# One activation table for logarithm and exponential, loaded by hand, in a two-layer decoder trunk

## The chip, the cores and the metric

The kernel runs on one core of a Trainium2 chip. The metric is device time in microseconds (us), from the start of the program to its end. Lower is better.

## The reference

One inference step of a two-layer hybrid decoder, for a prompt of 1024 tokens and for 8 samples of 4 tokens each (1056 tokens in all), with D_MODEL = 1024. Layer 0 has gated DeltaNet heads and a spatial-gating group in parallel, layer 1 has mLSTM heads. Each layer ends in a squared-ReLU MLP of width 4096. Cut to what matters here:

```python
def rmsnorm(x, g):
    y = x * lax.rsqrt(jnp.mean(x * x, -1, keepdims=True) + EPS)
    return y * g
# layer 0
q, k = l2norm(silu(conv(q))), l2norm(silu(conv(k))); v = silu(conv(v))
beta = sigmoid(beta_pre); g = -exp(a_log) * softplus(a_pre + dt_bias)
decay = exp(gc_i - gc_j)                      # per chunk, and exp(gc), exp(gc_last - gc)
o_a = rmsnorm(o, gdn_norm_g) * silu(gate)
u = gelu(u_pre); vb = rmsnorm(gelu(v_pre), sgu_norm_g)
# layer 1
bcum = cumsum(log_sigmoid(f_pre)); w_intra = exp(dmat - m_t); w_inter = exp(inter - m_t)
hh = rmsnorm(h, head_norm_g) * sigmoid(o_pre)
# every layer
x = x + rmsnorm(mix, gl[1])
x = x + rmsnorm(jnp.square(relu(rmsnorm(x, gl[2]) @ w1)) @ w2, gl[3])
```

The kernel computes every reciprocal square root on ScalarE (ACT) as `exp(-0.5 * ln(mean + eps))`: one `Ln` and one `Exp`. Softplus and log-sigmoid are `Abs`, `Exp` and `Ln`.

## The kernel before, in words

The tokens are in two groups: group 0 has 512, group 1 has 512 and the 32 of the samples. Each dense product is cut into units of 128 output columns (128x1024 weights, 512 KB). Weights and inputs are float32, and each is split into a high part and a rest, so a product is three matmuls (high x high, rest x high, high x rest). For a unit, SyncE (SP) starts the transfer of the weights into `wst`, ACT writes the high part `whi` (`hi`, L936 to L942, a `Copy` of 128x1024), VectorE (DVE) subtracts it and writes `wlo` (L1355), and TensorE (PE) multiplies (L488, a helper through which all matmuls go). `wst`, `whi` and `wlo` have two buffers each.

The class `Plan` writes one order by hand, a list of items, and every engine runs through the same list and does its own share of each item, in that order. A unit is in the list as 4 pieces, `("d", unit, piece)`. Between the pieces stand the items of the token mixers, which run on 128 tokens at a time (`gdn`, L1125 to L1190, for layer 0; `ml`, L1242 to L1267, for layer 1), and of the norms (`square`, `norm_sum`, `pre`). No engine takes its work out of this order, so what ACT does for a mixer or a norm also delays the `whi` and the emptying of dense results that stand behind it in the list. Engines wait for each other by semaphores.

ACT applies one function table set at a time. The program names only the functions. When it is built, a load of a table set (`ACT_TABLE_LOAD` in the trace) is put in front of each activation whose function the set then loaded lacks, and of the sets that hold this function the first in the list is taken. The first set with `Exp` has no `Ln`, and the first set with `Ln` has no `Exp`. `Silu`, `Gelu` and `Sigmoid` are each in sets of their own. `Copy`, `Square`, `Relu` and `Abs` are in every set that this kernel loads. A set further down the list, `natural_log_exp_and_others`, holds both `Ln` and `Exp`.

Where the functions are used on ACT:

- Norms over the model width (`norm_sum`, 16 of them): `Ln` L1065, `Exp` L1068.
- Gates (`softplus`): `Exp` L1095, `Ln` L1096; `gdn_prep`: `Sigmoid` L1103, `Exp` L1106, L1110, L1112, L1113, L1115.
- Layer 0, nine tiles (8 of the prompt and the sample tile): `Ln` L1148 and `Exp` L1149, twice a tile (step "sum"); `Exp` L1152, `Ln` L1157, `Exp` L1159, L1161, L1163 (step "dec"); `Ln` L1199, `Exp` L1200 (`out_squares`). For the tiles of group 1 also `Silu` L1136, `Gelu` L1139 (step "act"), `Silu` L1142, `Gelu` L1143 (step "gact").
- The input product of layer 0, group 0: `Silu` and `Gelu` at L977, `Silu` at L981. That of layer 1: `Sigmoid` at L977.
- Layer 1, nine tiles: `Exp` L1248, L1250; `Ln` L1271, `Exp` L1272 (`head_rms`). `ml_prep`: `Exp` L1228, L1233.

All of them are called through the name `A_`, which in the kernel before is `act.activation` itself.

Of the kernel before, what the change touches and what calls it, by code (L numbers as in the profile page):

```python
# [8 lines left out]
ACT = mybir.ActivationFunctionType  # L9
# [271 lines left out]
def build(nc, x_prompt, x_sample, state_gdn, state_gdn_conv, state_mlstm_c, state_mlstm_n, state_mlstm_m,  # L281
# [4 lines left out]
    with ctx:  # L286
        sems = {}

        def S(name):
            if name not in sems:  # L290
                sems[name] = ctx.enter_context(nc.semaphore(name))
            return sems[name]
# [122 lines left out]
        def out_of(key, g):  # L415
            b = PLAN.jobs[key]["bank"]
            return DB[:, b:b + 2, 0:272] if g else DB[:, b, 0:512]

        def like(v, g):

            return v[:, 0:GN[1]].rearrange("p (a n) -> p a n", a=2) if g else v[:, 0:GN[0]]
# [27 lines left out]
        def evac_wait(eng, key):  # L449
            sem, v = PLAN.jobs[key]["read"]  # L450
            eng.wait_ge(S(sem), v)
# [3 lines left out]
        @block.sync  # L455
        def _(sp):
            def x_load(t):
                if t >= 4:
                    sp.wait_ge(S("x_turned"), t - 3)
                sp.dma_start(x_tm[:, t % 4, :], x_prompt[0, t * P:(t + 1) * P, :])\  # L460
                    .then_inc(S(f"x_loaded{t % 4}"), 16)

            for t in range(4):
                x_load(t)
            sp.dma_start(x_tm[0:NS, 4, :], x_sample.rearrange("b s d -> (b s) d")).then_inc(S("x_loaded4"), 16)
            for u, (kind, l, g, a, k) in enumerate(PLAN.units):
                dst = wst[:, u % 2, :]
                if kind == "f2":
                    src = w_ff2[l][a * FK * P:(a + 1) * FK * P, 2 * k * P:2 * (k + 1) * P]
                    src = src.rearrange("(t p) n -> p t n", p=P)  # L470
                else:
                    w = {"in": w_in[l][0], "out": w_out[l][0], "f1": w_ff1[l]}[kind] if kind != "f1" else w_ff1[l]
                    c0 = (a * FK + k) * P if kind == "f1" else a * P
                    if kind == "in" and a >= GATE0 // P:
                        c0 += 2 * H
                    src = w[:, c0:c0 + P].rearrange("(t p) n -> p t n", p=P)
                if u >= 2:
                    sp.wait_ge(S("w_split"), u - 1)
                sp.dma_start(dst.rearrange("p (a b) -> p a b", a=src.shape[1]), src)\
                    .then_inc(S(f"w_loaded{u % 2}"), 16)  # L480
                if u == 1:
                    for t in range(4, TILES):
                        x_load(t)

        @block.tensor
        def _(pe):
# [107 lines left out]
            def gate(l, g):  # L594
                begin(("gate", l, g))
                b = PLAN.jobs["gate", l, g]["bank"]
                if g == 0:
                    pe.wait_ge(S("wg_split"), l + 1)
                for i, t in enumerate(range(*GT[g])):
                    _, c, n = tok(t)  # L600
                    for k in range(KT):
                        for q, (x, w) in enumerate(((hhi, wg_hi), (hlo, wg_hi), (hhi, wg_lo))):
                            last = mm(DB[0:n, b, i * 8:(i + 1) * 8], x[g][:, k, c], w[:, k, :],
                                      start=k == 0 and q == 0, stop=k == KT - 1 and q == 2)
                last.then_inc(S("job_done"), 1)
# [173 lines left out]
            def ml_prep(g, i):  # L779
                if i == 1:  # L780
                    pe.wait_ge(S("m_g"), g + 1)
                    for j, t in enumerate(range(*GT[g])):
                        n = tok(t)[2]
                        for part in range(2):
                            b, c = (part, j * P) if t < TILES else (2, part * NS)
                            last = pe.transpose(MB[0:H, b, c:c + n], cols[0:n, t, part, :], ident[0:n, 0:n])
                    last.then_inc(S("m_rows"), 1)
                elif i == 5:
                    pe.wait_ge(S("m_lw"), g + 1)
                    for j, t in enumerate(range(*GT[g])):  # L790
                        _, c, n = tok(t)
                        for q, r in enumerate((AR, LWR, MR)):
                            last = pe.transpose(MB[0:n, 3, j * 12 + 4 * q:j * 12 + 4 * q + 4], r[0:H, c],
                                                ident[0:H, 0:H])
                    last.then_inc(S("m_cols"), 1)
                    pe.wait_ge(S("m_keep"), g + 1)
                    nk = 4 + g * NB
                    for h in range(H):
                        last = mm(MB[:, 2, h * (4 + NB):h * (4 + NB) + nk], spread(h), KPR[0:H, 0:nk])
                    last.then_inc(S("m_cols"), 1)  # L800
# [119 lines left out]

        @block.scalar
        def _(act):
            A_ = act.activation

            steps_done = [0]

            def own(ins):

# [7 lines left out]
            def hi(u):  # L936
# [4 lines left out]
                act.wait_ge(S(f"w_loaded{u % 2}"), 16 * (u // 2 + 1))  # L941
                A_(whi[:, u % 2, :], wst[:, u % 2, :], ACT.Copy).then_inc(S("w_hi"), 1)  # L942

# [3 lines left out]
            def in_end(u, l, g, c):  # L947
                i = PLAN.in_rank[u]
                b, n = i % 2, GN[g]
                if l == 0 and c < NCONV:  # L950
# [7 lines left out]
                    if c == 0:  # L958
                        evac_wait(act, ("misc", "par"))
                    A_(like(pout2[:, b], g), out_of((u, 0), g), ACT.Copy, scale=par[:, 100 + c:101 + c])  # L960
                    if g == 0:
                        last = A_(row[:, 3:3 + n], DB[:, bank, 0:n], ACT.Copy)
                    else:
                        A_(row[:, 3:275], DB[:, bank, 0:272], ACT.Copy)
                        A_(row[:, 275:515], DB[:, bank + 1, 0:240], ACT.Copy)
                        last = A_(row[:, 515:XR].rearrange("p (b s) -> p b s", b=NB)[:, :, 3:3 + LS],
                                  DB[:, bank + 1, 240:272].rearrange("p (b s) -> p b s", b=NB), ACT.Copy)
# [366 lines left out]
        def _(dve):  # L1334
# [29 lines left out]
            def h1_rest(u):  # L1364

                f = PLAN.ff1_rank[u]
                _, l, g, a, k = PLAN.units[u]
                n = GN[g]
                r = relu2[:, f % 2, 0:n]
                dve.wait_ge(S("h1_hi"), f + 1)  # L1370
                TT(h1lo[:, k, 0:n], r, h1hi[:, k, 0:n].bitcast(F32), ALU.subtract)\  # L1371
                    .then_inc(S("h1_split"), 1)
# [803 lines left out]
```

## Time and profile before

| | |
|---|---|
| median of 3 runs | 3125.89 us (3123.27 to 3126.25) |
| the profiled execution | 3117.21 us, its span 3115.5 us |
| PE busy | 2866.9 us, 92% of the span |
| weight loads on PE | 2560.4 us, 82% |
| DVE busy | 1420.0 us, 46% |
| ACT busy | 1293.5 us, 42% |
| mean granted clock of PE | 0.943 |
| HBM | 256.02 MB read, 54.91 MB written, 100 GB/s |

The span runs from the first to the last instruction of the profiled execution; 1.7 us of its time lie around it. "Busy" is the time in which an engine has an instruction running. "Idle before" a group of instructions is the time that the engine stood still just before them, and the name behind the arrow is what ended that wait. The granted clock is the share of full speed that PE was given.

### The profile page before, as it was taken

To read this page: it belongs to the slowest core of one execution; us is meant where nothing else is said; L and a number is where in the kernel's file an instruction comes from. 1 tells how busy PE (TensorE), PEld (TensorE's weight loads), DVE (VectorE), ACT (ScalarE), POOL (GpSimd) and SP (SyncE) were. 2 spreads that over 40 slices of the span, in tenths; PEclk is the share of its full clock that TensorE was granted. 3 is DMA by queue.
4 is the path that set the end of the run, shared out by engine and by line. 5 is a ranking of instruction groups with operands and counts; after the bars stand their busy time and mean duration, and the time that the engine had idled before them with its cause. 6 is when DMAs were issued, how large, how long until landed. Compare 5 with 4: busy or idle time off the path is not lost.

```text
span 3115.5 us, 41770 instructions
## 1 busy us (share of the span) xinstructions
PE 2866.9 (92%) x17557; PEld 2560.4 (82%) x17557; DVE 1420.0 (46%) x2129; ACT 1293.5 (42%) x2055; POOL 213.3 (7%) x348
## 2 busy tenths in 40 slices
PE   6989998869999998999999999999999889999995
PEld 5769898758787866888999998998777678899995
DVE  4543555455444443543444446443444435544334
ACT  3564443755535442444234334343343225433322
POOL 4010010100000000010000000010000100000000
PEclk7998998979999998989999999899999999999998
DMA  4442232313222222443332233354334544233222
GB/s 140 130 119 76 80 90 69 103 63 95 63 86 64 82 85 77 143 152 122 102 95 75 89 102 109 119 159 129 89 102 113 113 85 145 88 104 121 86 85 77
DMA packets 365354, 313.64 MB, mean 101 GB/s; under 512 B 11153, under 2 KB 338859, under 8 KB 365168
## 3 DMA queue, kind: packets, MB, share of 16 engines
q1 hardware_dynamic: 335024, 205.68, 23.7%
q0 software_dynamic: 30144, 105.30, 10.6%
q8 instruction: 139, 2.28, 0.3%
q14 instruction: 47, 0.39, 0.0%
HBM read 256.02 MB, written 54.91 MB: 100 GB/s over the span
## 4 chain that ended last, share of the span: by engine, by line
PE 75%; ACT 10%; DVE 8%; issue 3%; DMA 3%; POOL 0%; SPq 0%; ACTq 0%; DVEq 0%; POOLq 0%
PE dense L488 63%; PE mixer L488 10%; DVE wlo L1355 2%; ACT whi L942 1%; DVE ffh L1394 1%; DMA out_dram<-arena 1%; ACT L1148 1%; DMA wst<-in_w_out_odd_dram 1%; DVE hf L1477 1%; DMA wst<-in_w_ff_dram 1%; DMA xl<-xd 1%; DVE ssum L1446 0%; ACT L1065 0%; ACT L1149 0%; ACT h1hi L1016 0%
## 5 line engine op out<-in xcount | busy, mean ns | idle before, releaser
L488 PE MATMUL dense<-hhi,whi 128*128 128x272 f32 (+1 forms) x3072 | 871.4, 338 | 63.0 <-DVE wlo L1355 39.4
L488 PE MATMUL dense<-hhi,wlo 128*128 128x272 f32 (+1 forms) x3072 | 840.6, 328 | 0.0
L488 PE MATMUL dense<-hlo,whi 128*128 128x272 f32 (+1 forms) x3072 | 840.1, 328 | 0.0
L1355 DVE TENSOR_TENSOR wlo<-wst,whi 128x1024 fp32r<-128x1024 f32 x384 | 470.3, 1225 | 450.9 <-ACT whi L942 450.7
L488 PEld LDWEIGHTS dense<-hhi,whi 128*128 128x128 f32 x3072 | 529.7, 194 | 129.4 <-DVE wlo L1355 49.1
L942 ACT ACTIVATE whi<-wst 128x1024 fp32r<-128x1024 f32 x384 | 404.1, 1052 | 482.9 <-PE dense L488 444.4
L488 PEld LDWEIGHTS dense<-hhi,wlo 128*128 128x128 f32 x3072 | 525.7, 193 | 44.5
L488 PEld LDWEIGHTS dense<-hlo,whi 128*128 128x128 f32 x3072 | 529.3, 194 | 39.9 <-issue 1.2
L488 PE MATMUL dense<-h1hi,whi 128*128 128x272 f32 (+1 forms) x1536 | 431.3, 335 | 28.8 <-DVE wlo L1355 18.9
L488 PE MATMUL dense<-h1hi,wlo 128*128 128x272 f32 (+1 forms) x1536 | 422.1, 329 | 0.0
L488 PE MATMUL dense<-h1lo,whi 128*128 128x272 f32 (+1 forms) x1536 | 420.2, 328 | 0.0
L488 PE MATMUL mixer<-arena 128*128 128x128 f32 (+5 forms) x2272 | 352.4, 305 | 73.5 <-DVE arena L1591 14.4
L488 PEld LDWEIGHTS mixer<-arena 128*128 128x128 f32 (+3 forms) x2272 | 302.4, 191 | 120.3 <-DVE arena L1591 15.4
L488 PEld LDWEIGHTS dense<-h1hi,whi 128*128 128x128 f32 x1536 | 262.6, 192 | 62.3 <-DVE wlo L1355 22.9
L488 PEld LDWEIGHTS dense<-h1hi,wlo 128*128 128x128 f32 x1536 | 263.0, 192 | 22.9
L488 PEld LDWEIGHTS dense<-h1lo,whi 128*128 128x128 f32 x1536 | 263.1, 192 | 21.2
L1371 DVE TENSOR_TENSOR h1lo<-relu,h1hi 128x544 fp32r<-128x544 f32 (+1 forms) x128 | 90.5, 707 | 393.9 <-ACT relu L1017 393.7
L1013 ACT ACTIVATE relu<-dense 128x544 f32<-128x544 f32 (+1 forms) x128 | 77.8, 608 | 354.0 <-PE dense L488 354.0
L1429 DVE TENSOR_TENSOR accA<-dense,accA 128x512 f32<-128x512 f32 (+1 forms) x168 | 116.6, 700 | 123.3 <-PE dense L488 123.1
L977 ACT ACTIVATE ffh<-dense 128x512 f32<-128x512 f32 (+1 forms) x72 | 43.9, 610 | 218.3 <-PE dense L488 218.2
L1446 DVE TENSOR_TENSOR ssum<-ssum,sq 128x512 f32<-128x512 f32 (+1 forms) x112 | 79.1, 706 | 88.1 <-ACT sq L1057 86.6
L1937 POOL DMA_DIRECT2D proj<-ffh x96 | 52.4, 546 | 683.4 <-ACT ffh L977 386.3
(351 smaller groups left out, 2296.9 us busy)
## 6 DMA issues: line engine op xcount, KB each, us to landing
wst<-in_w_ff_dram SPq DMA_DIRECT2D x256, 512.0 KB, 3.9
wst<-in_w_in_even_dram SPq DMA_DIRECT2D x48, 512.0 KB, 3.9
wst<-in_w_in_odd_dram SPq DMA_DIRECT2D x48, 512.0 KB, 3.9
proj<-ffh POOLq DMA_DIRECT2D x48, 272.0 KB, 2.4
proj<-ffh POOLq DMA_DIRECT2D x48, 256.0 KB, 2.3
arena<-proj POOLq DMA_DIRECT2D x8, 1536.0 KB, 9.9
xl<-xd POOLq DMA_DIRECT2D x32, 272.0 KB, 3.1
wst<-in_w_out_even_dram SPq DMA_DIRECT2D x16, 512.0 KB, 4.1
```

Of the source, the lines that this page charges most:

```text
L488: return pe.matmul(out, lhsT, rhs, start=start, stop=stop)
L942: A_(whi[:, u % 2, :], wst[:, u % 2, :], ACT.Copy).then_inc(S("w_hi"), 1)
L977: A_(like(pout2[:, b], g), out_of((u, 0), g), func).then_inc(S("act_evac"), 1)
L1013: A_(like(relu2[:, f % 2], g), out_of(key, g), ACT.Relu).then_inc(S("act_evac"), 1)
L1148: after(own(A_(rb, M4(1 - q)[:, :, 0:n], ACT.Ln, bias=epsc[:, :])))
L1355: TT(wlo[:, u % 2, :], wst[:, u % 2, :], whi[:, u % 2, :].bitcast(F32), ALU.subtract)\
L1371: TT(h1lo[:, k, 0:n], r, h1hi[:, k, 0:n].bitcast(F32), ALU.subtract)\
L1394: ins = STT(o, x, cw[j], o, ALU.mult, ALU.add)
L1429: TT(v, out_of(key, g), v, ALU.add).then_inc(S("dve_evac"), 1)
L1446: ins = TT(ssum[:, 0:n], ssum[:, 0:n], sq2[:, c % 2, 0:n], ALU.add)
L1477: STT(hf2[:, c % 2, 0:n], ACC(name, g)[:, c, :], gain(l, q, c), rstd[:, 0:n], ALU.mult, ALU.mult)\
L1937: dma(proj[l][c, :, G0[g]:G0[g] + n], pout2[:, i % 2, 0:n]).then_inc(S(f"stored{i % 2}"), 16)
```

## The change

`A_` becomes a function. It remembers in `logs[0]` whether the joint set is the one loaded. Before a `Ln` or an `Exp`, if it is not, it loads `natural_log_exp_and_others` by an instruction of its own and notes that. A `Silu`, `Gelu` or `Sigmoid` takes the note back. Every activation is then issued as before, with the same operands and in the same order, and no wait is added or removed.

```diff
         @block.scalar
         def _(act):
-            A_ = act.activation
-
-            steps_done = [0]
+            steps_done, logs = [0], [False]
+
+            def A_(out, in_, func, **how):
+
+                if func in (ACT.Ln, ACT.Exp) and not logs[0]:
+                    act.preload_act_table_set("natural_log_exp_and_others")
+                    logs[0] = True
+                elif func in (ACT.Silu, ACT.Gelu, ACT.Sigmoid):
+                    logs[0] = False
+                return act.activation(out, in_, func, **how)
```

## Rows read from the trace of the kernel before

**Rows 1.** Page: busy time, share and instructions of each engine; chain of waits by engine.
```profile
PE 2866.9 (92%) x17557; PEld 2560.4 (82%) x17557; DVE 1420.0 (46%) x2129; ACT 1293.5 (42%) x2055; POOL 213.3 (7%) x348
...
PE 75%; ACT 10%; DVE 8%; issue 3%; DMA 3%; POOL 0%; SPq 0%; ACTq 0%; DVEq 0%; POOLq 0%
```

**Rows 2.** PE's waits: engine, line, what ended them: us in total, times, longest.
```profile
PE dense L488 <- DVE wlo L1355: 58.4, 27, 7.4
...
PE mixer L488 <- DVE arena L1746: 11.2, 4, 2.8
...
PE mixer L488 <- DVE arena L1626: 9.9, 2, 6.7
```

**Rows 3.** ACT's groups: line, operation, count | busy us, mean ns | idle before, what ended it.
```profile
L942 ACT ACTIVATE whi<-wst 128x1024 fp32r<-128x1024 f32 x384 | 404.1, 1052 | 482.9 <-PE dense L488 444.4 <-DMA wst<-in_w_ff_dram 17.4 <-DMA wst<-in_w_out_odd_dram 11.3
...
L1148 ACT ACT_TABLE_LOAD x18 | 23.1, 1283 | 0.3
L1149 ACT ACT_TABLE_LOAD x18 | 23.1, 1283 | 0.3
L1065 ACT ACT_TABLE_LOAD x16 | 20.5, 1283 | 32.3 <-PE dense L488 32.3
L1068 ACT ACT_TABLE_LOAD x16 | 20.5, 1283 | 0.3
...
L977 ACT ACT_TABLE_LOAD x10 | 12.8, 1283 | 18.5 <-PE dense L488 18.4
...
L1157 ACT ACT_TABLE_LOAD x9 | 11.5, 1283 | 0.2
...
L1106 ACT ACT_TABLE_LOAD x1 | 1.3, 1283 | 0.0
```

**Rows 4.** ACT in order of time, 955.9 to 965: start, us, instruction.
```profile
955.98 0.63 ACT L1017 ACTIVATE relu<-relu 128x512 f32<-128x512 f32 x1
956.62 1.28 ACT L1148 ACT_TABLE_LOAD   x1
957.92 0.69 ACT L1148 ACTIVATE arena<-mixer,epsc 128x512 f32<-128x512 f32 x1
958.63 1.28 ACT L1149 ACT_TABLE_LOAD   x1
...
963.86 0.63 ACT L1149 ACTIVATE arena<-arena 128x512 f32<-128x512 f32 x1
964.40 1.04 ACT L942 ACTIVATE whi<-wst 128x1024 fp32r<-128x1024 f32 x1
```

**Rows 5.** DVE and PE in order of time, 965 to 968: in brackets idle before.
```profile
965.74 1.22 DVE L1355 TENSOR_TENSOR wlo<-wst,whi 128x1024 fp32r<-128x1024 f32 x1
...
967.01 0.80 PE L488 MATMUL dense<-hhi,whi 128*128 128x512 f32 x1 [5.20 <-DVE wlo L1355]
```

**Rows 6.** PE in order of time: first and last of 45 idle stretches.
```profile
32.67 0.77 PE L488 MATMUL dense<-hhi,whi 128*128 128x512 f32 x1 [4.99 <-DVE hlo L1473]
...
2638.00 0.47 PE L488 MATMUL dense<-hhi,whi 128*128 128x512 f32 x1 [3.29 <-ACT relu L1013]
```

**Rows 7.** DVE in order of time: behind a head norm, and behind the last norm.
```profile
2210.25 0.16 DVE L1771 TENSOR_TENSOR small<-small 128x4 f32<-128x4 f32 x1 [2.36 <-ACT small L1272]
...
3082.05 0.78 DVE L1458 SCALAR_TENSOR_TENSOR hf<-arena,par,rstd 128x544 f32<-128x544 f32 x1 [5.39 <-ACT rstd L1068]
```

**Rows 8.** Stretches: us, busy by engine, then PEclk, DMA share, GB/s.
```profile
390.00:393.00 3.00, 3.00 (x15) 3.00 (x14) 3.00 (x9) 2.95 (x11) 0.81 (x1) 0.50 0.45 117
803.00:806.00 3.00, 3.00 (x8) 2.32 (x8) 1.73 (x2) 1.06 (x1) 0.00 (x0) 0.50 0.02 5
...
2264.00:2268.00 4.00, 3.44 (x15) 2.94 (x16) 3.75 (x8) 1.38 (x2) 0.00 (x0) 1.00 0.05 6
2639.00:2642.00 3.00, 3.00 (x9) 2.34 (x8) 1.98 (x3) 1.68 (x3) 0.00 (x0) 0.52 0.03 7
```

## The prediction

> **What bounds the kernel now.** I read the page first. PE is busy 92% of the span, DVE 46%, ACT 42%, and the chain of waits gives PE 75%, ACT 10% and DVE 8% [rows 1]. So PE sets the time. ACT has much idle time, and time taken off it counts only where PE stands still for it, not per microsecond of ACT. The span of 3115.5 us less 2866.9 us of PE leaves 249 us in which PE has nothing running. That is the pool that this change can draw from.
>
> Next I read who PE waits for. The largest row is `wlo`, the rest of the weights, with 58.4 us in 27 waits. Mixer steps on DVE come next, with 11.2 and 9.9 us [rows 2]. None of these names ACT, but `wlo` comes from `whi`, which ACT writes, and ACT is in order.
>
> Then the groups of ACT. Table loads are 172 in number, at 23 lines, each 1283 ns: from L1148 and L1149 with 18 each down to L1106 with one [rows 3]. 172 x 1.283 = 220.7 us, a sixth of ACT's busy time. `whi` itself waits 482.9 us in all, of which 444.4 are for PE and about 29 for the two largest weight transfers [rows 3]: when ACT gets to a `whi`, PE or ACT itself is late, seldom the transfer.
>
> Last, ACT in order of time. Between a `Relu` that ends at 956.61 and the `whi` at 964.40 stand two `Ln` and two `Exp`, each with its load: load at 956.62, `Ln` at 957.92, load at 958.63 [rows 4]. PE waited 5.20 us for the `wlo` behind that `whi` [rows 5].
>
> **The change part by part.**
>
> *What goes.* I walked through ACT's activations in the order of the trace with the rule of the kernel's build (the first set that has the function), which gives the 172 loads at the very lines of the trace. With the rule of the change the same walk gives 55: the first one at L942 (1), those of `Silu`, `Gelu` and `Sigmoid` (37: L977 10, L981 5, L1136, L1139, L1142 and L1143 5 each, L1103 2), and 17 by hand (L1199 5, L1065 4, L1148 3, L1095 3, L1106 1, L1110 1). So 117 loads go: all 16 at L1068, all 18 at L1149, 15 of 18 at L1148, 12 of 16 at L1065, all 45 of L1157, L1159, L1200, L1271 and L1272, 4 of 9 at L1199, 4 at L1096, 2 at L1228 and one at L1110. In time 117 x 1.283 = 150 us of ACT. ACT should fall from 1293.5 to about 1143 us.
>
> *What is added.* The 17 loads by hand stand where a load stood before, right before the activation and behind its waits, so they cost nothing more (17 x 1.283 us are there already). No wait is added, no DMA moves, DVE, POOL and SP keep their order. A load from another set is taken to last as long: all 23 lines read 1283 ns, whichever set they load [rows 3]. I can't bound it better than by those, and with 17 loads even 0.5 us either way is under 9 us on ACT and half that on PE.
>
> *One load's price.* From load to activation is 1.30 us (956.62 to 957.92), and the load begins 0.01 us after the activation before ended [rows 4]. Without a load between them, the `whi` starts at 964.40, 0.09 us before the `Exp` of 963.86 has ended [rows 4]. So a load costs from 1.30 to 1.40 us; I take 1.28 in the sums below and add the rest once, as 3 us.
>
> The Trainium skill says otherwise (ScalarE: Activation LUTs, What ACT_TABLE_LOAD costs): 1283 ns for the load and some 1380 ns for a drain, 2.66 us for each switch. The load agrees to the nanosecond. The drain doesn't show in these rows, where the engine goes on after 0.01 us on either side. By the page the whole sum would be 2.05 times as large.
>
> *What of it PE sees.* For each idle stretch of PE over 0.1 us I followed the waits back through DVE and ACT to the PE instruction or transfer where they start, and added up the loads on the way that go. 45 stretches have some, from 32.67 to 2638.00 [rows 6], 122 us long in all. Of each I take the smaller of its length and its loads, since once the stretch is closed more speed is worth nothing. The stretch at 961.8 has five such loads (L1200, two each of L1148 and L1149), 6.4 us, against 5.20 of length [rows 4, 5], and counts 5.2. The 45 give 89.0 us, in three kinds:
> - Straight chains, 24.4 us in 10 stretches: four head norms in front of L1746 (2.57 each), the dense results that ACT empties behind a norm, as at 2638.00 [rows 6]. To these comes the tail: the last norm at 3078 has nothing beside it, DVE waits 5.39 us there [rows 7], 2.6 us of it two loads. Together 27.0. In a head norm DVE waits 2.36 us of the 2.57 [rows 7], because it has small steps of its own; so I take nine tenths, 24.3.
> - `wlo`, 32.6 us in 17 stretches. Here `whi` must also have its weights and DVE must be free. I take three quarters, 24.5.
> - Mixer steps of layer 0, 32.0 us in 18 stretches, long chains back and forth between ACT, DVE and PE. In these the step that is next late is the DVE step that runs beside ACT, or ACT's own work. Three quarters again, 24.0.
>
> Sum 72.8, with the 3 us from above 75.8. The ends are 24.3 (nothing but the first kind) and 91.6 (everything).
>
> *The clock.* PE's granted clock is 0.50, which is 1.2 of 2.4 GHz, in short stretches, many of them right after PE stood still: 390 to 393 behind the wait that ended at 388.4, 2639 to 2642 (0.52) behind that of 3.29 us [rows 6, 8]. There are 16 such stretches behind waits that mostly go, with 62.8 us of PE work in them, at half speed. At full speed that is 31.4 us less. But it isn't a law: 803 to 806 is at 0.50 with no wait before it, and 2264 to 2268 is at 1.00 right after a wait of 2.8 us [rows 8]. I take a little under half, 13 us.
>
> *What comes back.* A PE that is some 80 us quicker reaches other waits sooner. Where DVE or a transfer was just in time, a new wait opens. The waits that no load touches are about 112 us (234 us in waits over 0.02 us, less 122), and I let them grow by a tenth, 11 us.
>
> Result: 75.8 + 13 - 11 = 78 us. Against the profiled execution, 3117.2 - 78 = 3039 us. The median of the runs shown is 8.7 us above that execution, so against the median 3125.9 - 78 = 3048 us.
>
> **The rivals.**
>
> *The full account.* Every stretch closes and the clock comes back with it: 91.6 + 31.4 = 123 us, so 3003. For it: ACT gets 150 us, more than is asked for. Against: the row of 2.36 against 2.57, and stretches at half clock that have no cause in a wait.
>
> *DVE or the weights are next.* In the `wlo` and mixer stretches something else turns out to be nearly as late, and only a third of 64.6 comes, the clock nothing: 24.3 + 21.5 = 46 us, so 3080. For it: DVE ends most of PE's waits [rows 2], and its steps keep their length. Against: DVE is 46% busy [rows 1], and only some 29 us of `whi`'s waits are for weights [rows 3].
>
> *The loads by hand don't count.* If the build puts in its own loads without regard to those by hand, all 172 stay and 17 come on top, at norms and tiles of layer 0. Their price on ACT is 17 x 1.30 = 22 us, on PE by the share above (73 of 150) 11 us: 3137, slower. It decides at the count of loads in the trace, 189 and not 55; above 172 the kernel is slower. Nothing in the profile of before speaks for it, since it has no load by hand; against it stands that the build knows at each activation what is loaded (it puts no load before `Copy` or `Square`).
>
> *Nothing goes.* The build may order loads anew by runs and give what it gave before: 172 loads, 3126. The Trainium skill has such a rule (ScalarE activation tables: per-element evaluation and per-set limits, Table sets in the compiler and the runtime): the back end takes, per block, the set that serves the longest run. By that rule the `Ln` and `Exp` of a tile would already share a set in the kernel before, and there would be nothing to gain. The trace contradicts it, with 18 loads at L1148 and 18 at L1149 next to each other [rows 3, 4].
>
> *A switch costs more than its row.* If each load also held ACT for as long again as its row, inside the activations around it, 2 x 72.8 = 146 us would go: 2980. The start times in [rows 4], with the `Relu`, `Ln` and `Exp` at their usual 0.63 to 0.69 us, speak plainly against it. This is the case of the page ScalarE: Activation LUTs of the Trainium skill, above.
>
> **How the numbers follow.** Forecast 0.60 (3048, its own range 3025 to 3070), full account 0.10, DVE or weights next 0.22, loads by hand don't count 0.03, nothing goes 0.03, more than its row 0.02. The range for 8 in 10 goes from 3010 to 3090 and takes in the middle of the second and most of the third. About 0.2% (6 us) is what a measurement of this kernel can tell from no change. Faster has 0.94, same 0.03, slower 0.03.
>
> **What would show it.** Right: 55 table loads, ACT near 1143 us, none at L1068, L1149, L1200, L1272; PE's waits for `wlo` well under 58 us and for L1746 near zero; PE's idle time down by some 65 to 75 us and its granted clock a little above 0.943. If the loads are gone and `wlo` waits stay near 50, the third case holds. If PE's busy time falls by more than 25 us, I took the clock too small. I am wrong altogether if the count of loads is 172 or 189, or if the loads are gone and the time has moved by less than 30 us.

## The result, and the profile after

The changed kernel takes 3009.51 us (median of 4, 3002.10 to 3013.07), the kernel before 3125.39 us beside it. The ratio is 0.9627, 95% interval 0.9608 to 0.9646: 116 us faster. The forecast was 3048 us with a range from 3010 to 3090, so the kernel is faster, as was said, and the time lies just under the range. The gain is half as large again as the 78 us of the forecast.

The profiled execution took 3002.10 us. First the page after: span, busy time of each engine, and the chain of waits by engine.

```profile
span 3000.4 us, 41653 instructions
...
PE 2830.3 (94%) x17557; PEld 2536.0 (85%) x17557; DVE 1419.0 (47%) x2129; ACT 1144.3 (38%) x1938; POOL 212.3 (7%) x348
...
PE 82%; DVE 8%; ACT 5%; DMA 3%; issue 2%; SPq 0%; POOL 0%; ACTq 0%; DVEq 0%; POOLq 0%
```

ACT lost 149.2 us (1293.5 to 1144.3) and 117 instructions (2055 to 1938) [rows 1]. PE has the same 17557 matmuls, and two things changed on it. Its time without any matmul fell from 248.6 to 170.1 us, by 78.5. And its busy time fell by 36.6 us, with the same instructions: they ran at a higher clock (0.959 against 0.943). 78.5 + 36.6 = 115.1 us, the whole difference of the two executions. The share of ACT in the chain of waits halved, from 10% to 5% [rows 1].

The table loads after, from the groups of ACT (columns as in rows 3). L928 is now the load by hand, L932 the line of all activations, in front of which the build still puts its own loads:

```profile
L932 ACT ACT_TABLE_LOAD x38 | 48.8, 1283 | 18.4 <-PE dense L488 17.2 <-PEq L2172 0.8
L928 ACT ACT_TABLE_LOAD x17 | 21.8, 1283 | 14.5 <-PE dense L488 10.3 <-DVE cols L1530 3.6 <-PE mixer L488 0.3
```

38 + 17 = 55, as worked out from the order of the functions, and each still 1283 ns. PE's waits after (rows 2 are those of before; the DVE lines moved down by 7, L1355 to L1362, L1746 to L1753):

```profile
PE dense L488 <- DVE wlo L1362: 26.6, 16, 5.6
...
PE mixer L488 <- DVE arena L1753: 4.1, 4, 1.1
```

`wlo` fell from 58.4 us in 27 waits to 26.6 in 16, the head norms from 11.2 to 4.1 [rows 2]. The two waits for L1633, which was L1626 with 9.9 us, are down to 0.4 us. The place of [rows 4, 5] after, first ACT, then DVE and the matmul that had waited:

```profile
907.55 0.68 ACT L932 ACTIVATE arena<-mixer,epsc 128x512 f32<-128x512 f32 x1
908.26 0.63 ACT L932 ACTIVATE arena<-arena 128x512 f32<-128x512 f32 x1
908.79 0.67 ACT L932 ACTIVATE arena<-mixer,epsc 128x512 f32<-128x512 f32 x1
909.50 0.63 ACT L932 ACTIVATE arena<-arena 128x512 f32<-128x512 f32 x1
910.04 1.05 ACT L932 ACTIVATE whi<-wst 128x1024 fp32r<-128x1024 f32 x1
```

```profile
911.37 1.22 DVE L1362 TENSOR_TENSOR wlo<-wst,whi 128x1024 fp32r<-128x1024 f32 x1
...
913.14 0.40 PE L488 MATMUL dense<-hhi,whi 128*128 128x512 f32 x1
```

Two `Ln` and two `Exp` stand back to back, and `whi` starts 2.49 us after the first of them (910.04 less 907.55) and not 7.78 us after its load (964.40 less 956.62) [rows 4]. So the four loads there took 5.29 us, 1.32 us each from start to start. The matmul that waited 5.20 us [rows 5] has no wait in front of it.

The clock, at two places where PE had stood still and then ran at half speed. The wait of 3.17 us that ended at 388.37 in the kernel before is gone, and the matmuls that ran at half speed behind it now run from 379.7 to 381.6. The wait that ended at 2638.00 is down from 3.29 to 0.84 us, and the matmuls behind it now start at 2527.4 (columns as in rows 8):

```profile
379.00:382.00 3.00, 3.00 (x26) 2.88 (x26) 1.91 (x9) 2.50 (x12) 0.00 (x0) 1.00 0.80 219
2527.00:2530.00 3.00, 2.57 (x11) 2.18 (x12) 1.21 (x2) 2.94 (x5) 0.00 (x0) 1.00 1.00 315
```

In the first, PE does 26 matmuls in 3 us where it did 15, and its clock is 1.00 where it was 0.50 [rows 8]. Over the whole execution the stretches at half speed are 33, with 211 us of PE work in them, where the kernel before has 53 with 288 us. Half of the 77 us of work that left half speed is 39 us, near the 36.6 us by which PE's busy time fell.

### The profile page after: what moved, and what is told of

It is laid out like the page before. It is cut to its first block, busy times and chain, and to the rows that moved or that the text cites. A ratio compares the mean times of both kernels' runs of the same rounds, so it can differ in the third digit from the quotient of the medians.

```text
span 3000.4 us, 41653 instructions
## 1 busy us (share of the span) xinstructions
PE 2830.3 (94%) x17557; PEld 2536.0 (85%) x17557; DVE 1419.0 (47%) x2129; ACT 1144.3 (38%) x1938; POOL 212.3 (7%) x348
## 3 DMA queue, kind: packets, MB, share of 16 engines
q0 software_dynamic: 30144, 105.30, 11.1%
## 4 chain that ended last, share of the span: by engine, by line
PE 82%; DVE 8%; ACT 5%; DMA 3%; issue 2%; SPq 0%; POOL 0%; ACTq 0%; DVEq 0%; POOLq 0%
PE dense L488 68%; PE mixer L488 12%; DVE wlo L1362 2%; DVE ffh L1401 1%; ACT arena L932 1%; ACT whi L932 1%; DMA out_dram<-arena 1%; DVE hf L1484 1%; ACT ffh L932 1%; DMA wst<-in_w_out_odd_dram 1%; DVE ssum L1453 0%; ACT L932 0%; DMA xl<-xd 0%; DVE arena L1753 0%; DVE accA L1436 0%
## 5 line engine op out<-in xcount | busy, mean ns | idle before, releaser
L488 PE MATMUL dense<-hhi,whi 128*128 128x272 f32 (+1 forms) x3072 | 858.0, 334 | 28.9 <-DVE wlo L1362 15.5
L488 PE MATMUL dense<-hhi,wlo 128*128 128x272 f32 (+1 forms) x3072 | 831.9, 325 | 0.0
L488 PE MATMUL dense<-hlo,whi 128*128 128x272 f32 (+1 forms) x3072 | 830.8, 325 | 0.0
L1362 DVE TENSOR_TENSOR wlo<-wst,whi 128x1024 fp32r<-128x1024 f32 x384 | 470.3, 1225 | 443.7 <-ACT whi L932 443.6
L488 PEld LDWEIGHTS dense<-hhi,whi 128*128 128x128 f32 x3072 | 522.2, 191 | 90.1 <-issue 25.7
L932 ACT ACTIVATE whi<-wst 128x1024 fp32r<-128x1024 f32 x384 | 404.1, 1052 | 477.0 <-PE dense L488 441.4
L488 PEld LDWEIGHTS dense<-hlo,whi 128*128 128x128 f32 x3072 | 521.8, 191 | 38.2 <-issue 1.2
L488 PE MATMUL dense<-h1hi,whi 128*128 128x272 f32 (+1 forms) x1536 | 429.7, 334 | 18.7 <-DVE wlo L1362 11.0
L488 PEld LDWEIGHTS dense<-h1hi,whi 128*128 128x128 f32 x1536 | 261.3, 192 | 51.2 <-DVE wlo L1362 14.4
L932 ACT ACTIVATE relu<-dense 128x544 f32<-128x544 f32 (+1 forms) x128 | 78.1, 611 | 359.7 <-PE dense L488 359.7
L932 ACT ACTIVATE arena<-mixer 128x512 f32<-128x512 f32 (+8 forms) x186 | 74.6, 417 | 212.3 <-PE mixer L488 148.5
L932 ACT ACTIVATE ffh<-dense 128x512 f32<-128x512 f32 (+3 forms) x124 | 62.2, 525 | 231.4 <-PE dense L488 227.6
```

Source lines behind the costliest of these rows:

```text
L488: return pe.matmul(out, lhsT, rhs, start=start, stop=stop)
L932: return act.activation(out, in_, func, **how)
L1362: TT(wlo[:, u % 2, :], wst[:, u % 2, :], whi[:, u % 2, :].bitcast(F32), ALU.subtract)\
```

## The experiments

All times are medians. Every group of kernels ran beside the kernel before on the same chip, whose median was 3124.35, 3125.26 and 3125.45 us in the three groups.

**All loads put back, of the joint set.** A counter over the `Ln` and `Exp` calls and a list `AGAIN` of the 117 places:

```diff
+                elif func in (ACT.Ln, ACT.Exp) and calls[0] in AGAIN:
+                    act.preload_act_table_set("natural_log_exp_and_others")
```

> The changed kernel with the 117 loads put back at the places where they were, but all of the joint set (172 loads in all). My theory: the gain is the time of the loads and nothing else, so this takes as long as before, 3125 us, up to 7 us more because loads written by hand stand behind the waits in front of nine head norms; PE idle near 249 us, granted clock near 0.943. Rival: part of the gain comes from which table is loaded or from the activations under it; then it stays under 3100 us.

Measured 3134.75 us, ratio 1.0033 (1.0020 to 1.0046), PE idle 253.0 us, clock 0.939. The whole gain is gone, and 10 us more, where I had allowed for 7. So the gain is the time of the loads, not another table or other activations. A load of the set that is there already costs the same as any other, as the groups of ACT say:

```profile
L932 ACT ACT_TABLE_LOAD x117 | 150.1, 1283 | 37.4 <-PE dense L488 26.1 <-DVE small L1780 9.0 <-DVE cols L1536 0.4
```

**28 loads put back, those in no chain that ended in an idle stretch of PE.** The same edit with a shorter `AGAIN`; the 28 are 5 each at L1065 and L1068, 3 at L1200, 2 each at L1148, L1149, L1096, L1228, L1271 and L1272, and one each at L1157, L1159 and L1110 (lines of the kernel before).

> The changed kernel with 28 loads put back, those that lay in no chain of waits that ended in an idle stretch of PE. My theory (a load costs only where PE stands still for it): within 8 us of the changed kernel, 3008 to 3018 us, PE idle 170 to 178 us, clock as in the changed kernel, 0.95 to 0.96. Rival (each load is worth the same, 116 us over 117 loads): 28 us more, 3037 us.

Measured 3015.80 us, ratio 0.9654 (0.9639 to 0.9668). The changed kernel beside it is at 3008.25, so 28 loads, 35.9 us of ACT, cost 7.6 us, 0.27 us each. The intervals of the two overlap (the changed kernel has 0.9616 to 0.9648), so even this small price is hardly clear of scatter. The equal worth of each load would have made 28 us, and that is ruled out. The page of this kernel:

```profile
PE 2837.8 (94%) x17557; PEld 2536.8 (84%) x17557; DVE 1419.8 (47%) x2129; ACT 1180.2 (39%) x1966; POOL 213.3 (7%) x348
```

ACT is 35.9 us busier than the changed kernel's 1144.3 beside it, and PE's idle time is 173.6 against 169.0.

**The other 89 put back.**

> The complement: 89 loads put back, those in a chain of waits that ended in an idle stretch of PE. My theory: nearly all of the gain goes, 3110 to 3125 us, PE idle 235 to 250 us and the clock back at 0.943 (half-speed stretches follow PE's waits). Rival (each load worth the same): 88 us more than the changed kernel, 3097 us. If the clock has to do with something else than PE's waits it stays at 0.955 and the time is near 3095.

Measured 3130.05 us, ratio 1.0019 (1.0008 to 1.0031): 121.8 us more than the changed kernel, 1.37 us a load, more than the load's own 1.28. PE is idle for 254.8 us, 85.8 more than the changed kernel, and busy for 40.5 more:

```profile
PE 2876.0 (92%) x17557; PEld 2566.4 (82%) x17557; DVE 1420.2 (45%) x2129; ACT 1258.0 (40%) x2027; POOL 212.6 (7%) x348
```

The two parts add up: 7.6 + 121.8 = 129.4 us, against 126.5 for all at once. Which loads lay on chains that ended in an idle stretch of PE was read from the one trace of before, and it parts loads worth 0.27 us from loads worth 1.37 us. What the expectation missed is that the kernel is slower than the one before, with 28 loads less. The last experiment takes that up.

**The changed kernel again, on the same chip.**

> The changed kernel once more on the same chip as the three others, so that they have a common measure: 3002 to 3013 us, ratio to the kernel before 0.961 to 0.965. Half-speed stretches of PE should again be fewer than in the kernel before (33 against 53 there), if they go with the waits and not with the execution.

Measured 3008.25 us, ratio 0.9632 (0.9616 to 0.9648), PE idle 169.0 us and busy 2835.5, 37 stretches at half speed. In the third group it was 3010.49 us (0.9628), idle 170.4, busy 2839.7, 38 stretches. The idle time repeats within 1.4 us, while PE's busy time, with the clock, moves by 9 us between executions. So in these three profiles (with the first one: idle 170.1, busy 2830.3) most of the scatter is that of PE's busy time.

**PE made to wait by DVE, not by ACT.** In `head_scale`, between the wait for the norm and its use, on a tile `spare` that nothing else reads:

```diff
                 dve.wait_ge(S("g_ossr"), mixed("ossr", t + 1))
+                for _ in range(6):
+                    link(TT(spare[:, :], spare[:, :], spare[:, :], ALU.mult))
                 link(TT(small[0:n, 7, :], small[0:n, 5, :], small[0:n, 2, :], ALU.mult))
```

> The changed kernel with six more DVE multiplications of 128x256 on a spare tile in each of the nine head norms (some 2.4 us each time), right where two table loads had made PE wait; ACT and its loads are untouched. It asks whether the half-speed stretches of PE go with PE's waits, whoever makes them. Theory: PE idle 15 to 22 us more than the changed kernel's 169, and PE busy 6 to 12 us more through the clock (half a microsecond per microsecond of wait, as in e3_on_back), together 3030 to 3042 us. Rival (the clock has to do with ACT's loads or with the execution): PE busy as in the changed kernel, 2835, and 3023 to 3030 us.

Measured 3041.73 us, ratio 0.9734 (0.9720 to 0.9747), 33 us more than the changed kernel of the first group. PE's idle time is 194.1 us, 25.1 more than the changed kernel's 169.0, and its busy time 14.8 more, with ACT's at 1144.4 as before. Both are above what I had expected (15 to 22, and 6 to 12). The six multiplications took longer than I had reckoned, 2.73 us:

```profile
1612.01 2.73 DVE L1782 TENSOR_TENSOR spare<-spare 128x256 f32<-128x256 f32 x6 [0.60 <-ACT small L933]
```

```profile
PE 2850.3 (94%) x17557; PEld 2551.1 (84%) x17557; DVE 1442.0 (47%) x2184; ACT 1144.4 (38%) x1938; POOL 212.2 (7%) x348
```

No load came or went here, and PE still lost 0.59 us of clock for each microsecond of wait. In the 89 loads it was 40.5 for 85.8, which is 0.47, and from before to after 36.6 for 78.5, again 0.47. These figures for whole executions carry the scatter of 9 us in the busy time. It is left out when only the part with eight of the nine head norms is compared, the same 5000 matmuls of the changed kernel and of this one (columns as in rows 8):

```profile
1503.51:2280.82 777.31, 763.29 (x5003) 705.49 (x5001) 363.65 (x530) 282.69 (x482) 41.16 (x58) 0.98 0.38 110
```

```profile
1505.87:2314.90 809.03, 775.67 (x5002) 715.81 (x5001) 383.67 (x579) 282.91 (x482) 41.04 (x58) 0.96 0.36 106
```

PE waits 33.4 us and not 14.0 there, and is busy for 12.4 us more, 0.64 for each microsecond of wait. In the two other profiles of the changed kernel its busy time for these matmuls is 763.3 and 764.7 us, so 12.4 is far outside the scatter. The kernel before has 32.7 us of waits and 774.1 us of busy time there: 10.8 us for 18.7, or 0.58. So the clock goes with PE's waits, whether ACT or DVE makes them.

**Every load by hand, ahead of the waits.** `A_` calls a helper `table(func)`, which knows five functions and loads by name. The steps call it before their waits, too:

```diff
             def norm_sum(e):
                 g = NORMS[e][2]
                 n = GN[g]
+                table(ACT.Ln)
                 if e:
                     act.wait_ge(S("n_stt"), KT * e)
```

> The changed kernel with the same 55 loads, but each by hand and ahead of the waits of its activation instead of behind them, so that ACT loads while it waits. In the changed kernel 14 loads have idle time of ACT before them, 14.0 us of it at most of use. My theory: PE sees a half to all of that, 6 to 13 us faster than the changed kernel, 2996 to 3003 us, PE idle 160 to 165 us (169 in the changed kernel). Rival: those waits are for PE, which has other pieces to do meanwhile, so nothing moves (3008 us).

Measured 3002.40 us, ratio 0.9606 (0.9593 to 0.9619). The changed kernel has 0.9632 and 0.9628, so this is some 6 to 8 us faster, but the intervals touch. Two of PE's waits near the start shrank, in this profile and in that of the next kernel alike: the one for `hlo` behind the first norm from 4.99 to 3.71 us, and one for ACT's `ffh` from 3.75 to 1.9. But other waits were longer, a wait for `wlo` at 2425 us among them (6.3 us, and 3.8 to 4.2 in the changed kernel), so that the idle time is 169.1 us, as without the edit, and not the 160 to 165 that I had expected. I call the gain in time likely, not shown.

**Gelu ahead of Silu in the gate step,** on top of that: 53 loads.

> As e4_before_waits, and in the gate step of a group 1 tile of layer 0 the Gelu stands ahead of the Silu, so that the Silu that opens the next tile finds its set loaded: 53 loads instead of 55. Theory: 0 to 4 us faster than e4_before_waits (two loads, where PE may wait or not). Rival: no change beyond 0.1%.

Measured 3002.63 us, ratio 0.9608 (0.9594 to 0.9621). No change: what these two loads cost PE is less than the times can tell.

**The Gelu units of the input product together,** on top of both: 51 loads.

```diff
-SEQ_A = [0, 20, 1, 21, 2, 22, 3, 4, 5, 6, 7, 8, 9, 10, 11, 23]
+SEQ_A = [0, 20, 21, 22, 1, 2, 3, 4, 5, 6, 7, 8, 9, 10, 11, 23]
```

> As e5_gelu_first, and in the input product of layer 0 the three Gelu units 20, 21 and 22 stand together behind unit 0, no longer between convolution units: 51 loads. Theory: two loads less give 0 to 3 us, but the convolution units 1 and 2 come closer together, whose DVE work is then less covered; net within 5 us of e5_gelu_first. Rival: the convolution sets the pace there and it is over 5 us slower.

Measured 2994.37 us, ratio 0.9581 (0.9568 to 0.9595), 8 us under the one before it in this list, where I had expected no more than 5. It was run once more beside the changed kernel:

> e7_gelu_units once more, now beside the changed kernel on one chip, to see if it really beats it: ratio to the kernel before 0.957 to 0.960, 10 to 15 us under the changed kernel.

> The changed kernel on the same chip as e7_again and e8_back_ahead: 3005 to 3012 us, ratio 0.962 to 0.9645.

Measured 2991.65 us, ratio 0.9570 (0.9557 to 0.9583), and the changed kernel 3010.49, ratio 0.9628 (0.9615 to 0.9642). This one beats both kernels, by 19 us and 134 us; the 19 are more than the 10 to 15 expected. Most of it comes at the start, as two stretches show, of the changed kernel and then of this one:

```profile
0.00:100.00 100.00, 68.97 (x302) 57.28 (x303) 33.36 (x54) 35.41 (x52) 36.06 (x94) 0.78 0.39 115
100.00:200.00 100.00, 89.22 (x366) 69.69 (x365) 58.64 (x88) 61.92 (x89) 11.10 (x19) 0.95 0.51 156
```

```profile
0.00:100.00 100.00, 74.82 (x341) 61.66 (x342) 39.25 (x61) 39.52 (x59) 36.68 (x94) 0.80 0.45 130
100.00:200.00 100.00, 91.77 (x411) 72.52 (x410) 64.89 (x105) 69.22 (x119) 15.37 (x22) 0.98 0.50 152
```

PE does 752 matmuls in the first 200 us and not 668. How much of that is the two loads, the loads ahead of the waits, or the order of the units by itself, these runs don't part.

**The 89 loads back, ahead of the wait in the head norms.** Why was the kernel with 144 loads slower than the one with 172? In the kernel before, the load in front of a `Ln` ran while DVE still did its small steps, and the `Ln` waited for them. A load by hand takes over the wait that stands in front of it. Seven of the nine head norms have their loads back in that kernel; the loads of the two others are among the 28. DVE and ACT in a head norm of the kernel with 89 loads back:

```profile
2203.13 0.16 DVE L1780 TENSOR_TENSOR small<-small 128x4 f32<-128x4 f32 x1
...
2206.46 0.16 DVE L1782 TENSOR_TENSOR small<-small 128x4 f32<-128x4 f32 x1 [3.17 <-ACT small L936]
```

```profile
2203.32 1.28 ACT L932 ACT_TABLE_LOAD   x1 [0.82 <-DVE small L1780]
2204.61 0.30 ACT L936 ACTIVATE small<-small,epsc 128x4 f32<-128x4 f32 x1
```

The load waits 0.82 us for a DVE result that only the `Ln` needs, and DVE waits 3.17 us where it had waited 2.36 [rows 7]. All seven read 3.17. The edit moves that load ahead of the wait:

```diff
             def head_rms(t, n):
+                early[0] = calls[0] in AGAIN
+                if early[0]:
+                    act.preload_act_table_set("natural_log_exp_and_others")
                 act.wait_ge(S("g_msq"), t + 1)
```

> e3_on_back with the same 144 loads, but in the nine head norms the load in front of the logarithm stands ahead of its wait for DVE, where the build had put it in the kernel before. It asks why e3_on_back is slower than the kernel before with 28 loads less. Theory (a load behind a wait can't lie under it; 0.82 us in each head norm): PE idle 3 to 7 us less than e3_on_back's 254.8, DVE's wait in the head norm back from 3.17 to 2.36 us, and 3122 to 3127 us. Rival (the difference is scatter): time as e3_on_back, 3130 us.

The loads are back in seven head norms in both kernels, not in nine. Measured 3123.98 us, ratio 1.0002 (0.9987 to 1.0017), against 1.0019 (1.0008 to 1.0031) with the load behind the wait. DVE's wait is back where it was:

```profile
2202.41 0.16 DVE L1786 TENSOR_TENSOR small<-small 128x4 f32<-128x4 f32 x1 [2.36 <-ACT small L936]
```

PE's waits for the head norms (L1757 and L1761, the old L1746) are 14.4 us with the load behind the wait and 11.2 with it ahead, as in the kernel before [rows 2]:

```profile
PE mixer L488 <- DVE arena L1757: 14.4, 4, 3.6
```

```profile
PE mixer L488 <- DVE arena L1761: 11.2, 4, 2.8
```

Three more of PE's waits behind head norms fell by 0.8 us each, so the seven give 5.6 us, within the 3 to 7 expected. That settles the wait. With the changed kernel beside it at 3010.49 us, the 89 loads now cost 113.5 us, 1.28 us each, in place of 1.37. Of the times, the intervals overlap by a little, so that difference is likely and not more. The idle time as a whole fell by 11.1 us. 4.1 of them are one wait for the transfer of the mLSTM state, which has nothing to do with the edit. The first norm, below, is another place where a load by hand costs more than the one that it replaces: PE's wait behind it is 6.27 us in both kernels and 4.99 in the kernel before.

## Why the prediction was wrong, by its own steps

**The counts: right.** 55 loads, ACT at 1144.3 us where 1143 was said, none left at the lines named.

**The price of a load: right.** 149.2 us of ACT's busy time over 117 loads is 1.275 us. Time around a load would not be in that, but it would be in the 1.32 us from start to start, measured at the place of [rows 4], and in the whole gain. The Trainium skill (ScalarE: Activation LUTs, What ACT_TABLE_LOAD costs) gives 2.66 us a switch, with its drain; by that, an estimate, the four loads there would have taken 10.6 us, and they took 5.29. The 1283 ns that the Trainium skill gives there for the load itself stand in every row. This answers the rival "a switch costs more than its row", too.

**What PE sees: right in sum, and in kind.** The matmuls are the same in the same order, so each wait can be compared with itself:

| kind | of the loads in it | taken | measured |
|---|---|---|---|
| straight chains, with the tail | 27.0 | 24.3 | 22.3 |
| `wlo` | 32.6 | 24.5 | 26.2 |
| mixer steps of layer 0 | 32.0 | 24.0 | 26.6 |
| overlap of activations | | 3 | in the above |
| sum | 91.6 | 75.8 | 75.1 |

The straight chains gave less than taken since in the head norms the first of the two loads had lain under DVE's steps for 0.82 us, and so was worth only 0.46. I had seen DVE's wait of 2.36 us [rows 7] and read it as the gain; it was 1.76, as the same row after says, with 0.60 us left:

```profile
2110.07 0.16 DVE L1778 TENSOR_TENSOR small<-small 128x4 f32<-128x4 f32 x1 [0.60 <-ACT small L932]
```

For the same reason "they cost nothing more" was wrong for two of the 17 loads by hand. At L1110 the load of before began at 186.07 and was over before DVE's result came at 189.67. After, it waits 3.65 us for that result and then loads:

```profile
185.65 1.28 ACT L928 ACT_TABLE_LOAD   x1 [3.65 <-DVE cols L1530]
```

The other is the first norm, before and after:

```profile
24.57 1.28 ACT L1065 ACT_TABLE_LOAD   x1
27.72 0.69 ACT L1065 ACTIVATE rstd<-dense,epsc 128x512 f32<-128x512 f32 x1 [1.86 <-PE dense L488]
```

```profile
28.29 1.28 ACT L928 ACT_TABLE_LOAD   x1 [3.15 <-PE dense L488]
```

There the load at L1068 went, and the one at L1065 came out from under its wait. PE's wait of 4.99 us, the first of the 45 [rows 6], is 4.99 us in the changed kernel, too. With the load by hand ahead of the wait it is 3.71.

**What comes back: wrong, by 14 us.** I let the waits that no load touches grow by 11 us, since a quicker PE would find transfers or DVE late. The 63 of them shrank instead, by 7.3 us (2.7 of it is the tail, counted above), and four new ones have 1.2 us together. There was no ground for the 11 in any row: DVE was 46% busy and ACT had just lost 149 us. The largest part is a wait for `wlo` that went from 7.41 to 3.75 us.

**The clock: the step that failed.** "I take a little under half, 13 us" of 31.4 was the largest error, 23.6 of the 37 us by which the forecast missed. PE's busy time fell by 36.6 us in the profiled execution, and by 31.4 and 27.2 in the two other profiles of the changed kernel, against the one profile of the kernel before. For each microsecond of wait that went, that is 0.47, 0.39 and 0.35 us. The matmuls that had run in the stretches I had named (seventeen by the same rule, not sixteen) took 27.9 us less, and in the others 29.4 and 27.8: nearly all of the 31.4. What is left, 8.7, 2.0 and -0.6 us, is different in each execution. I had cut the term because of two stretches that didn't follow the rule [rows 8], one without a wait before it and one wait without a stretch after it. They were no reason to halve the rest, since the named stretches gave nearly all of it. The one without a wait, 803 to 806, was not even of the kernel: its matmuls took 2.89 us in the one profile of before and 1.62 us, at full speed, in all three of the changed kernel and also with 117 and with 89 loads back. The experiment with DVE's waits shows the dependence: from a third to two thirds of a microsecond of clock for each microsecond of wait.

So the failure is of size, not of mechanism: the clock term and the term for what comes back. With 0.47 us of clock for each of the 75.8 us, and nothing for what comes back, the same working gives 75.8 + 35.6 = 111 us (with hindsight, since the 0.47 is measured here). The rival "full account" (3003 us, chance 0.10) had the clock right and the waits too large. "DVE or the weights are next" is refuted by the table, and "the loads by hand don't count" and "nothing goes" by the count of 55. The rule for the second of these, the longest run (Trainium skill, ScalarE activation tables: per-element evaluation and per-set limits, Table sets in the compiler and the runtime), is not what placed the loads of this kernel: the 18 loads at L1148 and 18 at L1149 of the kernel before speak against it [rows 3], and the walk with the first set gave the 55 right. The range was said to take in the middle of the full account, but that is at 3003 us, below its lower end of 3010; the measured 3009.51 lies between the two.

## What to carry to other kernels

Sum table loads only where the chain of waits behind them ends in an idle stretch of the engine that sets the time: here that parted loads worth 1.3 to 1.4 us from loads worth 0.27 us. Then add what the clock gives back, here 0.35 to 0.47 of what PE no longer waits over the whole execution, and don't discount it for single exceptions. Name the table set by hand where two functions alternate and one set has both, and put that load ahead of the activation's wait, not between the two.

## What the runs showed of the hardware

- PE's clock follows its waits, whether ACT or DVE makes them: over the same 5000 matmuls, 19.4 us more of waits made by DVE alone cost 12.4 us more of PE's busy time, and 18.7 us more with the loads of the kernel before cost 10.8.
- A load of the set that is already loaded is not skipped: 117 of them took 1283 ns each and brought the whole 126 us back.
- A load can lie under its activation's wait. With the load between wait and activation, DVE waited 3.17 us and not 2.36 in each of seven head norms.
- The time without matmuls repeats within 1.4 us between three profiles of the changed kernel (169.0 to 170.4), while PE's busy time scatters by 9 us (2830.3 to 2839.7).
